# A two-block model on one core: order of two roots, banks of the sums between layers, weight loads three ahead, smaller pieces in the mixing stages, and reordered growth

## The chip, the cores and the metric

The kernel runs on one core of a Trainium2 chip. The metric is the device time of one execution in microseconds (us), lower is better. The comparison is between the median of several executions of the kernel before and of the kernel with the change.

## The reference, cut to what matters

The input is a sequence of 1024 tokens with 1024 channels in f32. The first block computes three branches from one normed input (a WKV7 recurrence, a gated convolution of width 31, an attention to 256 memory rows), merges them with three gates, projects, adds the input and norms with `g_final`. The second block has two layers, and the change lies in it and in what joins it to the first:

```
for layer in range(2):
    h = rms_norm_2(x, norm_pre[layer])
    proj = h @ w_in[layer]                       # 32 tiles of 128 columns and one of 32
    y_a = gla_branch(...)                        # 4 heads, gated scan in both directions
    y_b = diff_branch(...)                       # 4 heads: (softmax(q1 k1) - lam softmax(q2 k2)) v, then norm and gate
    y_c = hgrn_branch(...)                       # 4 heads of 64, gated scan in both directions
    y = concatenate([y_a, y_b, y_c]) @ w_out[layer]
    x = x + rms_norm_2(y, norm_post[layer])
```

## The kernel before, in words

**Engines and the plan.** One Python list, `plan`, is written out by generators, and each engine (TensorE, ScalarE, VectorE, GpSimd, and SyncE, which issues most DMAs) walks through that list and issues its own part of every step. So the order of the plan is the order on every engine, and an engine that waits in one step holds up all its later steps. The profile calls the engines PE (with PEld for its weight loads), ACT, DVE, POOL and SP. A `Filler` (L139) wraps a generator and advances it by fractions of a step; `weave` (L160) advances fillers beside a main generator.

**Projections.** `P` (L331) multiplies the normed input, kept as a rounded f32 part `hh` and a bf16 rest `hl`, by one weight tile: 48 matmuls of 128x512, three products (hh by wh, hh by wl, hl by wh). `deep=4` puts 12 matmuls into one step of the plan. Each projection holds a pair of PSUM banks until a later step copies it out. Banks 0 to 3 are `LOWER` (two pairs), 4 to 7 are `UPPER`. A weight tile comes by DMA into one of two staging slots (SP), ACT copies it into one of three split slots (`wh`), and POOL writes the rest (`wl`). `fill` (L909) decides where in the plan a `load` stands: as early as a split slot is free, but for at most two projections beyond the one that has begun (L921, L934). A slot is free from the step with the last matmuls of its projection; the copy on ACT waits for those.

**End of the first block.** `closing` (L660) runs the last eight projections, squares each result on ACT (`stat_sq`) and adds the squares on DVE. Matmuls with a matrix of ones (`stat_most`, `stat_sum`) add over the channels. For the tag `fin` there are two sums: `fin`, whose root belongs to the first block's norm, and `pre0`, whose root serves the second block's first norm. `stat_end` (L1562) takes Ln and Exp of one sum on ACT. Before the change `pre0` is summed and rooted first. Then `norm_pre` (DVE, L2041) and `split` (ACT, then POOL or DVE) make the input `p0`, and the projections begin. `norm_fin` (DVE) writes the first block's result and SP stores it, for use at the end of layer 0.

**Between the layers.** After the closing projections of layer 0, `resid` adds the layer's result to the input, and `stat("pre1", S)` squares and sums it in a pair of `LOWER` banks; that pair is free after the last `norm_pre` of layer 1.

**The mixing stage** (`mix`, L853), once per layer. Two chains run woven into each other, and a third kind of work fills in:
- `attend` (L816) goes through 4 heads x 8 blocks of 128 queries. Per block: `qk` (PE, 4 matmuls of 128x512 f32), two `dmax` (DVE), two `dexp` (ACT, exponentials with sums), `dw` (DVE: reciprocal, a small product, a scaling of 128x1024 by a column, and one fused multiply-add), then for this block one round later `dt` (PE, 8 transposes), `WT` (ACT, two copies), `dv` (PE) and `do` (ACT).
- `scan` (L681) does the gated scans for t = 0 (gla, 4 heads of 32) and t = 1, 2 (hgrn, 2 heads of 64 each). For each t there are seven levels. A level is: `xk` (ACT, two copies of 128x512), `lev` (PE, 4 parts for t = 0, else 2, each of 8 matmul pairs, in a pair of `LOWER` banks), `leve` (DVE, a predicated copy per part) and `grow` (DVE, six products: for each direction the keys, the queries, and the tree of gates). `xk` and `lev` of the next level wait for all six.
- `beside` (L807) makes values, queries and keys of the next head (`dv_ready`, `qk_ready`) and finishes earlier heads (`head_out`), by projections with `deep=4`. How fast it and `scan` advance beside the blocks is set by hand in `PACE` and `BESIDE` (L844, L845).

Of the kernel before, what the change touches and what calls it, by code (L numbers as in the profile page):

```python
# [135 lines left out]
class Filler:  # L136
# [5 lines left out]
    def step(self, n=1.0):  # L142
        self.owed += n
        while self.owed >= 1 and self.live:
            self.owed -= 1
            try:
                next(self.g)
            except StopIteration:
                self.live = False
# [11 lines left out]
def weave(main, *fillers):  # L161
    for stage in main:
        for f, *n in fillers:
            f.step(n[min(stage or 0, len(n) - 1)])


def build(nc, ctx, A, out):
# [163 lines left out]
    def P(key, src, h, n=S, m=128, back=False, among=LOWER, deep=2):  # L331
# [5 lines left out]
        for part in range(steps // deep):  # L337
            yield
# [317 lines left out]
    def closing(tag, w, h):  # L656
# [16 lines left out]
        for t in tags[::-1]:  # L673
# [100 lines left out]
    def dv_ready(L, h):  # L774

        yield from P(("dvp", L, h), A["w_in_2"][L][14 + h], f"p{L}", deep=4)
        do("dv_copy", L, h)
        yield
        two(("dv_turn", L, h), ("dv_turn", L, h))

    def qk_ready(L, h):

        for i in range(2):
            yield from P(("dqk", L, h, i), A["w_in_2"][L][6 + 4 * i + h], f"p{L}", deep=4)
            do("dq_copy", L, h, i)
            yield
            held(("rope", L, h, i), ("rope", L, h, i))
            yield
# [3 lines left out]
    def head_out(L, h):  # L792
# [6 lines left out]
        yield from between(P(("dg", L, h), A["w_in_2"][L][18 + h], f"p{L}", deep=4), None, ("do_norm", L, h))  # L799
# [14 lines left out]
    def attend(L, n):  # L814
# [15 lines left out]
        if n < 32:  # L830
            do("dw", L, h, q)
        yield
        if n:
            for g in range(2):
                do("WT", L, *last, g)
        yield
        if n:
# [7 lines left out]
    BESIDE = ((1, 2, 3, 2, 3, 3, 3, 2), (5, 6, 4, 3, 0, 0, 1, 6), (3, 4, 3, 4, 3, 1, 0, 0), (0, 2, 3, 3, 3, 2, 2, 0))  # L845
# [7 lines left out]
    def mix(L):  # L853
        ahead, pace = Filler(scan(L)), PACE
        first = Filler(norms_fin() if L == 0 else iter(()))
        for g in (dv_ready(L, 0), qk_ready(L, 0)):
            weave(g, (ahead, 1.2), (first, 2.0))
        for n in range(33):
# [3 lines left out]
            for _ in attend(L, n):  # L862
                ahead.step(pace[h])
                other.step(BESIDE[h][q] / 6)
                ahead.step(pace[h])
            if q == 7:
# [5 lines left out]
    for L in range(2):  # L872
        do("small_load", L)
        if L:
            run(stat("pre1", S))
# [13 lines left out]
    for stage, names in (  # L889
# [8 lines left out]
            ("diff", "dv_copy dv_turn dq_copy rope turned qk dmax dexp dw dt WT dv do do_sq do_sum do_rs do_norm dg_sig dg_out")):  # L898
# [22 lines left out]
    fill(2)  # L921
    for i, s in enumerate(plan):
# [11 lines left out]
        fill(begun + 2)  # L934
# [18 lines left out]
    def tensor_program(pe):  # L953
# [373 lines left out]
        def lev(L, t, lv, g, p):  # L1327
# [3 lines left out]
            if (g, p) == (0, 0):  # L1331
# [4 lines left out]
                else:  # L1336
                    pe.wait_ge(*at("grow", L, t, lv - 1))
# [9 lines left out]
        def kt(L, t, d, g):  # L1347
            use = ("kt", L, t, d, g)
            cleared(use)
            pe.wait_ge(*at("grow", L, t, 6))  # L1350
# [171 lines left out]
    def scalar_program(act):  # L1522
# [375 lines left out]
        def xk(L, t, lv):  # L1898
# [5 lines left out]
            else:  # L1904
                if lv > 1:
                    act.wait_ge(*at("lev", L, t, lv - 2, 1, 1 if t == 0 else 0))
                act.wait_ge(*at("grow", L, t, lv - 1))
# [74 lines left out]

        def WT_(L, h, q, g):
# [28 lines left out]
        def dg_sig(L, h):  # L2012
# [10 lines left out]
                    sg_sig=sg_sig, dv_copy=dv_copy, dv_turn=dv_turn, dq_copy=dq_copy, dexp=dexp, WT=WT_, do=do_, do_sq=do_sq,  # L2023
# [12 lines left out]
    def vector_program(dve):  # L2036
# [396 lines left out]
        def grow(L, t, lv):  # L2433
# [4 lines left out]
            m = 1 << lv  # L2438
            for d in range(2):
# [455 lines left out]
```

## Time and profile before

| | us |
|---|---|
| median of three runs (lowest, highest) | 4501.37 (4494.43, 4509.14) |
| the profiled execution's own time | 4500.21 |
| its span in the trace | 4498.4 |
| mean granted TensorE clock of that execution | 0.931 of full speed |

The profiled execution lies within 1.2 us of the median, and its span leaves 1.8 us around it. In the profile the first block takes until about 2418 us, the mixing stage of layer 0 about 2440 to 3350, that of layer 1 about 3490 to 4450. Times in a timeline are counted from the span's start. In its rows the number behind the start is the length of the merged piece, the brackets give the idle time of that engine before it and what ended it. Matmuls in plain f32 stand as two instructions each.

### The profile page before, as it was taken

The page shows a single profiled execution, that of the slowest core. Times are in us where ns is not written, and L with a number is a line of the kernel's source. Part 1 is how long each engine was busy: PE and PEld are TensorE (multiplying, and loading weights), DVE is VectorE, ACT ScalarE, POOL GpSimd, SP SyncE. Part 2 cuts the span into 40 slices and gives each one's busy share as a digit, 9 for nine tenths or more (in the row PEclk, how much of TensorE's full clock was granted, in tenths as well). Part 3 has the DMA queues.
Part 4 walks back from the last instruction along what each step waited for, and adds up shares of the span by engine and source line. Part 5 has one row for each costly group of instructions (what it writes and reads, how often), then busy time and mean ns, then how long its engine had stood idle before and what let it go on. Part 6 is the DMA issues. An engine that isn't in the chain of part 4 may idle for free.

```text
span 4498.4 us, 66792 instructions
## 1 busy us (share of the span) xinstructions
PE 3923.6 (87%) x29404; PEld 2409.6 (54%) x29404; DVE 1992.3 (44%) x2165; ACT 1439.2 (32%) x1795; POOL 958.7 (21%) x426
## 2 busy tenths in 40 slices
PE   6988899999989999988997978988787978978777
PEld 3555565666656665455444555555444455555444
DVE  2456455555454642432224354263642264264542
ACT  4222323233232322222113323333444232343442
POOL 2313333232333322031132201111002210111002
PEclk8999999999999999999998988989888989989899
DMA  2111111111111112432212000100012100100002
GB/s 92 53 39 39 48 39 53 39 53 45 43 50 42 57 49 84 159 122 103 104 69 86 30 10 19 33 15 24 19 52 76 34 10 10 43 19 20 24 8 101
DMA packets 61585, 226.93 MB, mean 50 GB/s; under 512 B 6832, under 2 KB 8560, under 8 KB 60784
## 3 DMA queue, kind: packets, MB, share of 16 engines
q1 hardware_dynamic: 50064, 181.77, 11.7%
q10 hardware_dynamic: 11232, 40.90, 2.3%
q8 instruction: 231, 3.78, 0.3%
q14 instruction: 58, 0.48, 0.0%
HBM read 174.93 MB, written 47.71 MB: 49 GB/s over the span
## 4 chain that ended last, share of the span: by engine, by line
PE 71%; DVE 16%; ACT 9%; DMA 2%; issue 1%; POOL 1%; ACTq 0%; DVEq 0%; SPq 0%; POOLq 0%
PE psum L955 69%; DVE arena L2038 6%; ACT arena L1524 5%; DVE arena L2041 4%; DVE arena L2493 2%; DVE arena L2430 2%; PE psum L958 2%; ACT L1524 1%; ACT wh L1524 1%; DMA arena<-in_w_proj_conv 1%; DVE arena L2045 1%; ACT arena L1979 1%; DVE hl L2038 0%; ACT hh L1524 0%; POOL wl L2548 0%
## 5 line engine op out<-in xcount | busy, mean ns | idle before, releaser
L955 PE MATMUL psum<-arena 64*64 64x32 f32 (+11 forms) x19116 | 1589.3, 283 | 390.4 <-ACT arena L1524 186.2
L955 PEld LDWEIGHTS psum<-arena 64*64 64x64 f32 (+5 forms) x19116 | 1109.5, 158 | 878.5 <-issue 448.8
L2548 POOL TENSOR_TENSOR wl<-arena,wh 128x1024 bf16<-128x1024 f32 (+1 forms) x195 | 474.7, 2434 | 2405.4 <-ACT wh L1524 2403.6
L955 PE MATMUL psum<-hh,wh 128*128 128x512 f32 x3120 | 891.4, 432 | 98.6 <-ACT arena L1524 24.7
L1524 ACT ACTIVATE arena<-psum 128x512 f32<-128x512 f32 (+4 forms) x660 | 415.8, 630 | 1393.7 <-PE psum L955 1055.3
L955 PE MATMUL psum<-hh,wl 128*128 128x512 bf16 x3120 | 784.0, 394 | 1.2 <-POOL wl L2548 1.2
L955 PEld LDWEIGHTS psum<-hh,wh 128*128 128x128 f32 x3120 | 607.0, 200 | 301.7 <-issue 58.6
L2038 DVE TENSOR_TENSOR arena<-psum,arena 128x512 f32<-128x512 f32 (+3 forms) x488 | 319.3, 654 | 973.7 <-PE psum L955 628.1
L955 PE MATMUL psum<-hl,wh 128*128 128x512 bf16 x3120 | 736.0, 383 | 5.6 <-POOL hl L2548 5.5
L2041 DVE SCALAR_TENSOR_TENSOR arena<-arena 128x1024 f32<-128x1024 f32 x356 | 573.9, 1612 | 83.1 <-ACT arena L1524 69.9
L2548 POOL TENSOR_TENSOR arena<-arena 128x1024 f32<-128x1024 f32 (+4 forms) x142 | 362.6, 2553 | 955.1 <-ACT arena L1524 467.9
L955 PEld LDWEIGHTS psum<-hl,wh 128*128 128x128 bf16 x3120 | 301.7, 99 | 382.2 <-issue 30.2
L955 PEld LDWEIGHTS psum<-hh,wl 128*128 128x128 bf16 x3120 | 277.2, 97 | 414.3 <-issue 98.9
L2038 DVE TENSOR_TENSOR arena<-arena 128x512 f32<-128x512 f32 (+9 forms) x478 | 361.9, 757 | 265.9 <-ACT arena L1524 139.9
L1524 ACT ACTIVATE wh<-arena 128x1024 fp32r<-128x1024 f32 (+1 forms) x195 | 205.1, 1052 | 819.9 <-PE psum L955 538.0
L1524 ACT ACTIVATE arena<-arena 128x1024 f32<-128x1024 f32 (+3 forms) x282 | 253.3, 898 | 389.3 <-DVE arena L2038 217.3
L2493 DVE TENSOR_REDUCE arena<-psum 128x1 f32<-128x1024 f32 x128 | 156.8, 1225 | 318.8 <-PE psum L955 310.8
L2041 DVE SCALAR_TENSOR_TENSOR arena<-psum,arena 128x1024 f32<-128x1024 f32 (+2 forms) x73 | 83.3, 1141 | 412.2 <-ACT arena L1524 251.1
L1524 ACT ACT_TABLE_LOAD x151 | 193.7, 1283 | 57.7 <-PE psum L955 39.2
L1979 ACT ACTIVATE arena<-psum,arena 128x1024 f32<-128x1024 f32 x128 | 142.6, 1114 | 204.3 <-DVE arena L2493 195.9
L958 PE MATMUL psum<-arena 128*128 128x128 f32 x928 | 144.6, 302 | 55.8 <-ACT arena L1524 18.6
L2430 DVE COPY_PREDICATED arena<-arena,psum 128x1024 f32<-128x1024 int32 x112 | 148.7, 1327 | 66.7 <-PE psum L955 60.9
(38 smaller groups left out, 834.1 us busy)
## 6 DMA issues: line engine op xcount, KB each, us to landing
arena<-in_w_in SPq DMA_DIRECT2D x161, 512.0 KB, 3.5
scr_g<-arena ACTq DMA_DIRECT2D x24, 512.0 KB, 2.6
arena<-scr_g SPq DMA_DIRECT2D x24, 512.0 KB, 4.4
arena<-in_w_out SPq DMA_DIRECT2D x24, 512.0 KB, 3.5
arena<-in_w_mem_kv SPq DMA_DIRECT2D x16, 512.0 KB, 3.5
scr_x<-arena SPq DMA_DIRECT2D x16, 512.0 KB, 3.6
arena<-scr_x SPq DMA_DIRECT2D x16, 512.0 KB, 7.4
arena<-in_x SPq DMA_DIRECT2D x8, 512.0 KB, 10.3
```

What stands on the lines that cost most here:

```text
L955: return pe.e.matmul(o, l, r, start=start, stop=stop)
L958: return pe.e.matmul(o, i, ident if idn is None else idn, start=True, stop=True, is_transpose=True)
L1524: return act.seq.activation(o, i, func, bias=bias, scale=scale)
L1979: act.seq.activation(EX[z] if c == 0 else EX[2], pair(use), AF.Exp, bias=s[:, c:c + 1], scale=-1.0, accum_out=s[:, 4 + c:5 + c]).then_inc( ...
L2038: return dve.seq.tensor_tensor(o, a, b, op)
L2041: return dve.seq.scalar_tensor_tensor(o, a, s, b, op0, op1)
L2045: return dve.seq.tensor_scalar(o, a, s1, None, op0)
L2430: dve.seq.copy_predicated(AT8(p, g), mk, cols3(pair(use), 8)).then_inc(*dve.up("ATl", *use))
L2493: dve.seq.tensor_reduce(s[:, c:c + 1], pair(use), AX.X, MIN).then_inc(*dve.up("dmax", L, h, q, c))
L2548: return pool.seq.tensor_tensor(o, a, b, op)
```

## The change

1. In `closing` the sums and roots are made for `fin` first and then for `pre0`. `consts2`, the DMA that overwrites their buffers, now waits for the sum of `pre0`.
2. `stat("pre1")` between the layers takes its pair of banks from `UPPER`.
3. `fill` may place loads for three projections beyond the one begun. The numbers of slots (two staging, three split) stay.
4. In the mixing stages the projections of `beside` use `deep=1`, 3 matmuls per step, each step counted as a quarter; the other steps of `dv_ready` and `qk_ready` that only wait count as a half. `beside` is advanced twice per step of `attend`, by half each time, and `BESIDE` has new numbers. `first` (the first block's `norm_fin`) begins two steps earlier.
5. `dw` is split: `dr` (DVE, the reciprocal and the small product), `e1` (ACT, the scaling of 128x1024, which was on DVE) and `dw` (DVE, the fused multiply-add). They stand in three successive steps of `attend`; `e1` stands behind `WT` of the block before.
6. In `grow` the six products go keys, keys, queries, queries, tree, tree. `xk` waits for the second, `lev` for the fourth; the transposes `kt` wait for the second.

```diff
     def step(self, n=1.0):
         self.owed += n
         while self.owed >= 1 and self.live:
-            self.owed -= 1
             try:
-                next(self.g)
+                self.owed -= next(self.g) or 1
 ...
 def weave(main, *fillers):
-    for stage in main:
-        for f, *n in fillers:
-            f.step(n[min(stage or 0, len(n) - 1)])
+    for share in main:
+        for f, n in fillers:
+            f.step(n * (share or 1))
 ...
-        for t in tags[::-1]:
+        for t in tags:
             do("stat_sum", t)
             do("stat_end", t)
 ...
     def dv_ready(L, h):
-        yield from P(("dvp", L, h), A["w_in_2"][L][14 + h], f"p{L}", deep=4)
+        yield from P(("dvp", L, h), A["w_in_2"][L][14 + h], f"p{L}", deep=1, share=0.25)
         do("dv_copy", L, h)
-        yield
+        yield 0.5
         two(("dv_turn", L, h), ("dv_turn", L, h))
 ...
-            yield from P(("dqk", L, h, i), A["w_in_2"][L][6 + 4 * i + h], f"p{L}", deep=4)
+            yield from P(("dqk", L, h, i), A["w_in_2"][L][6 + 4 * i + h], f"p{L}", deep=1, share=0.25)
             do("dq_copy", L, h, i)
-            yield
+            yield 0.5
             held(("rope", L, h, i), ("rope", L, h, i))
-            yield
+            yield 0.5
 ...
-        yield from between(P(("dg", L, h), A["w_in_2"][L][18 + h], f"p{L}", deep=4), None, ("do_norm", L, h))
+        yield from between(P(("dg", L, h), A["w_in_2"][L][18 + h], f"p{L}", deep=1, share=0.25), None, None, None, ("do_norm", L, h))
 ...
         if n < 32:
-            do("dw", L, h, q)
+            do("dr", L, h, q)
         yield
         if n:
             for g in range(2):
                 do("WT", L, *last, g)
+        if n < 32:
+            do("e1", L, h, q)
         yield
+        if n < 32:
+            do("dw", L, h, q)
 ...
-    BESIDE = ((1, 2, 3, 2, 3, 3, 3, 2), (5, 6, 4, 3, 0, 0, 1, 6), (3, 4, 3, 4, 3, 1, 0, 0), (0, 2, 3, 3, 3, 2, 2, 0))
+    BESIDE = ((1, 1.9, 2.1, 2.1, 2.1, 2.2, 2.4, 2.6), (5, 5, 4, 3, 0, 0, 4, 4), (3, 3, 3, 3, 2, 1, 1, 1.4), (1, 2, 3, 3, 3, 2, 2, 0))
 ...
         first = Filler(norms_fin() if L == 0 else iter(()))
+        first.step(2)
 ...
                 ahead.step(pace[h])
-                other.step(BESIDE[h][q] / 6)
+                other.step(BESIDE[h][q] / 12)
                 ahead.step(pace[h])
+                other.step(BESIDE[h][q] / 12)
 ...
         if L:
-            run(stat("pre1", S))
+            run(stat("pre1", S, UPPER))
 ...
-    fill(2)
+    fill(3)
 ...
-        fill(begun + 2)
+        fill(begun + 3)
 ...
-                    pe.wait_ge(*at("grow", L, t, lv - 1))
+                    pe.wait_ge(*at("grow_q", L, t, lv - 1, 1))
 ...
-            pe.wait_ge(*at("grow", L, t, 6))
+            pe.wait_ge(*at("grow_k", L, t, 6, 1))
 ...
-                act.wait_ge(*at("grow", L, t, lv - 1))
+                act.wait_ge(*at("grow_k", L, t, lv - 1, 1))
 ...
+        def e1(L, h, q):
+            z = q % 2
+            act.wait_ge(*at("dr", L, h, q))
+            f(EX[z], EX[z], AF.Copy, scale=DST[:, 16 * z + 6:16 * z + 7]).then_inc(*act.up("e1", L, h, q))
 ...
+            T, n = [tree(d, lv) for d in range(2)], 512 >> lv
             for d in range(2):
-                T = tree(d, lv)
-                tt(half(KG[d], d, m), half(KG[d], d, m), T[:, :, 1 - d:2 - d].to_broadcast([128, 512 >> lv, m]), MUL).then_inc(*dve.up("grow_k", L, t, lv, d))
-                tt(half(QF[d], 1 - d, m), half(QF[d], 1 - d, m), T[:, :, d:d + 1].to_broadcast([128, 512 >> lv, m]), MUL).then_inc(*dve.up("grow_q", L, t, lv, d))
-                x = tt(tree(d, lv + 1, True).unsqueeze(2), T[:, :, 0:1], T[:, :, 1:2], MUL)
-                x.then_inc(*dve.up(*(("grow", L, t, lv) if d else ("grow_0", L, t, lv))))
+                k = half(KG[d], d, m)
+                tt(k, k, T[d][:, :, 1 - d:2 - d].to_broadcast([128, n, m]), MUL).then_inc(*dve.up("grow_k", L, t, lv, d))
+            for d in range(2):
+                q = half(QF[d], 1 - d, m)
+                tt(q, q, T[d][:, :, d:d + 1].to_broadcast([128, n, m]), MUL).then_inc(*dve.up("grow_q", L, t, lv, d))
+            for d in range(2):
+                tt(tree(d, lv + 1, True).unsqueeze(2), T[d][:, :, 0:1], T[d][:, :, 1:2], MUL).then_inc(*dve.up("grow_t", L, t, lv, d))
 ...
-        def dw(L, h, q):
+        def dr(L, h, q):
             z = q % 2
             s = DST[:, 16 * z:16 * z + 16]
             dve.wait_ge(*at("dexp", L, h, q, 1))
             dve.seq.reciprocal(s[:, 6:8], s[:, 4:6]).then_inc(*dve.up("dw_rec", L, h, q))
-            tt(s[:, 8:9], s[:, 7:8], sc[:, 4:5], MUL).then_inc(*dve.up("dw_lam", L, h, q))
-            ts(EX[z], EX[z], s[:, 6:7], None, MUL).then_inc(*dve.up("dw0", L, h, q))
+            tt(s[:, 8:9], s[:, 7:8], sc[:, 4:5], MUL).then_inc(*dve.up("dr", L, h, q))
+
+        def dw(L, h, q):
+            z = q % 2
+            s = DST[:, 16 * z:16 * z + 16]
+            dve.wait_ge(*at("e1", L, h, q))
             stt(EX[z], EX[2], s[:, 8:9], EX[z], MUL, ADD).then_inc(*dve.up("dw", L, h, q))
 ...
         def consts2():
-            sp.wait_ge(*at("stat_sum", "fin"))
+            sp.wait_ge(*at("stat_sum", "pre0"))
```

## Rows read from the trace of the kernel before

**Rows 1.** The page: busy time, share of the span and instructions of each engine.
```profile
PE 3923.6 (87%) x29404; PEld 2409.6 (54%) x29404; DVE 1992.3 (44%) x2165; ACT 1439.2 (32%) x1795; POOL 958.7 (21%) x426
```
**Rows 2.** Busy time by stretch: first block, mixing stage of layer 0, of layer 1.
```profile
core 0: us, PE busy (x) PEld busy (x) DVE busy (x) ACT busy (x) POOL busy (x), PEclk, DMA share, GB/s
0.00:2400.00 2400.00, 2208.18 (x19607) 1360.06 (x19608) 1074.22 (x1067) 662.18 (x816) 674.51 (x307) 0.97 0.19 66
2540.00:3340.00 800.00, 650.56 (x4013) 415.75 (x4012) 389.19 (x484) 301.26 (x406) 80.01 (x33) 0.87 0.06 18
3540.00:4440.00 900.00, 746.51 (x4487) 466.38 (x4486) 415.59 (x504) 340.56 (x444) 106.45 (x45) 0.90 0.08 27
```
**Rows 3.** PE's groups by shape, 2540 to 3340: busy, mean | idle before, releasers.
```profile
L955 PE MATMUL psum<-arena 64*128 64x128 f32 x512 | 45.6, 326 | 49.9 <-ACT arena L1524 31.6 <-DVE arena L2430 13.3 <-DVE arena L2041 3.5
L955 PE MATMUL psum<-arena 32*128 32x128 f32 x512 | 43.7, 326 | 33.2 <-ACT arena L1524 16.8 <-DVE arena L2430 13.8 <-DVE arena L2038 2.6
```
**Rows 4.** Timeline of layer 0, t = 0: `lev`, a piece, `dt`, growth, `xk`.
```profile
2691.66 1.16 PE L955 MATMUL psum<-arena 32*128 32x128 f32 x16 [1.25 <-ACT arena L1524]
...
2696.66 2.77 PE L955 MATMUL psum<-hl,wh 128*128 128x512 bf16 x12
...
2706.72 1.10 PE L958 MATMUL psum<-arena 128*128 128x128 f32 x8 [0.63 <-ACT arena L1979]
...
2706.89 3.28 DVE L2038 TENSOR_TENSOR arena<-arena 128x512 f32<-128x512 f32 x6
...
2710.26 1.29 ACT L1524 ACTIVATE arena<-arena 128x512 f32<-128x512 f32 x2 [2.26 <-DVE arena L2038]
...
2711.69 1.57 PE L955 MATMUL psum<-arena 32*128 32x128 f32 x16 [3.88 <-ACT arena L1524]
...
2715.55 2.08 PE L955 MATMUL psum<-arena 32*128 32x128 f32 x16 [2.29 <-DVE arena L2430]
```
**Rows 5.** DVE's and ACT's groups by shape, 2540 to 3340.
```profile
L2430 DVE COPY_PREDICATED arena<-arena,psum 128x1024 f32<-128x1024 int32 x56 | 74.3, 1327 | 35.0 <-PE psum L955 32.1
L2038 DVE TENSOR_TENSOR arena<-arena 128x512 f32<-128x512 f32 x90 | 62.3, 692 | 43.1 <-PE psum L955 39.5 <-DVE arena L2493 0.5
...
L2045 DVE TENSOR_SCALAR arena<-arena 128x1024 f32<-128x1024 f32 x40 | 29.9, 747 | 45.2 <-ACT arena L1524 43.9
...
L1524 ACT ACTIVATE wh<-arena 128x1024 fp32r<-128x1024 f32 x24 | 25.4, 1059 | 17.0 <-PE psum L955 8.6 <-DMA arena<-in_w_in 6.5
L1524 ACT ACTIVATE arena<-arena 128x1024 f32<-128x1024 f32 x23 | 24.3, 1058 | 8.8 <-DVE arena L2038 5.9 <-DVE arena L2041 2.3
```
**Rows 6.** Timeline between the layers.
```profile
3475.77 1.06 ACT L1524 ACTIVATE hh<-arena 128x1024 fp32r<-128x1024 f32 x1 [1.35 <-DVE arena L2041]
...
3489.14 1.02 ACT L1524 ACTIVATE hh<-psum 128x1024 fp32r<-128x1024 f32 x1 [1.60 <-DVE psum L2041]
...
3489.17 1.22 PE L955 MATMUL psum<-hh,wh 128*128 128x512 f32 x2 [18.19 <-DVE psum L2041]
```
**Rows 7.** Timeline between the blocks, from the two squares to the first projections.
```profile
2416.64 2.24 ACT L1524 ACTIVATE arena<-arena 128x1024 f32<-128x1024 f32 x2 [12.45 <-DVE arena L2038]
...
2423.19 1.09 ACT L1524 ACTIVATE psum<-psum,arena 128x1024 f32<-128x1024 f32 x1 [2.95 <-PE psum L955]
...
2426.67 1.28 ACT L1524 ACT_TABLE_LOAD   x1
...
2430.39 1.06 ACT L1524 ACTIVATE arena<-arena 128x1024 f32<-128x1024 f32 x1
...
2432.76 1.19 PE L955 MATMUL psum<-hh,wh 128*128 128x512 f32 x2 [7.90 <-ACT hh L1524]
```
**Rows 8.** Timeline, start of the mixing stage of layer 0.
```profile
2467.64 1.06 ACT L1524 ACTIVATE wh<-arena 128x1024 fp32r<-128x1024 f32 x1 [8.64 <-DMA arena<-in_w_in]
...
2469.86 3.65 PE L958 MATMUL psum<-arena 128*128 128x128 f32 x16 [13.68 <-ACT arena L1524]
```
**Rows 9.** PE's groups of the first block, 0 to 2400: hh by wh.
```profile
L955 PE MATMUL psum<-hh,wh 128*128 128x512 f32 x1795 | 503.7, 427 | 47.5 <-ACT wh L1524 12.8 <-ACT hh L1524 9.6 <-DVE arena L2038 9.3
```

More of the change, by code:

```diff
@@ L329, in do, with P @@
         plan.append(step)
-    def P(key, src, h, n=S, m=128, back=False, among=LOWER, deep=2):
+    def P(key, src, h, n=S, m=128, back=False, among=LOWER, deep=2, share=None):
         PROJ[key] = (src, h, n, m, back)
@@ L337, in P @@
         for part in range(steps // deep):
-            yield
+            yield share
             if part == 0:
@@ L783, in qk_ready @@
         for i in range(2):
-            yield from P(("dqk", L, h, i), A["w_in_2"][L][6 + 4 * i + h], f"p{L}", deep=4)
+            yield from P(("dqk", L, h, i), A["w_in_2"][L][6 + 4 * i + h], f"p{L}", deep=1, share=0.25)
             do("dq_copy", L, h, i)
-            yield
+            yield 0.5
             held(("rope", L, h, i), ("rope", L, h, i))
-            yield
+            yield 0.5
             do("turned", L, h, i)
@@ L897, in build @@
                      " so_copy so_sum so_rs so_norm sg_sig sg_out"),
-            ("diff", "dv_copy dv_turn dq_copy rope turned qk dmax dexp dw dt WT dv do do_sq do_sum do_rs do_norm dg_sig dg_out")):
+            ("diff", "dv_copy dv_turn dq_copy rope turned qk dmax dexp dr e1 dw dt WT dv do do_sq do_sum do_rs do_norm dg_sig dg_out")):
         for name in names.split():
@@ L2022, in scalar_program @@
                     ga_copy=ga_copy, ga_abs=ga_abs, ga_ln=ga_ln, ga_exp=ga_exp, hz_gate=hz_gate, xk=xk, kt=kt, so_copy=so_copy, so_rs=so_rs,
-                    sg_sig=sg_sig, dv_copy=dv_copy, dv_turn=dv_turn, dq_copy=dq_copy, dexp=dexp, WT=WT_, do=do_, do_sq=do_sq,
+                    sg_sig=sg_sig, dv_copy=dv_copy, dv_turn=dv_turn, dq_copy=dq_copy, dexp=dexp, e1=e1, WT=WT_, do=do_, do_sq=do_sq,
                     do_rs=do_rs, dg_sig=dg_sig)
@@ L2536, in vector_program @@
                     norm_pre=norm_pre, small=small, ga_z=ga_z, ga_min=ga_min, hz_gate=hz_gate, hz_f=hz_f, ks=ks_, diage=diage, qf=qf, leve=leve,
-                    grow=grow, st=st, so_norm=so_norm, sg_out=sg_out, turned=turned, dmax=dmax, dw=dw, do_norm=do_norm,
+                    grow=grow, st=st, so_norm=so_norm, sg_out=sg_out, turned=turned, dmax=dmax, dr=dr, dw=dw, do_norm=do_norm,
                     dg_out=dg_out, resid=resid)
```

## The prediction

> **What bounds the kernel now.** I read the page first: PE is busy for 87% of the span, DVE for 44%, ACT for 32%, POOL for 21% [rows 1]. So the time is PE's work plus what PE waits for, and a busy microsecond on another engine counts only where PE waits for it. The view of busy time by stretch says where PE waits. In the first block it is busy for 2208 of 2400 us, at a granted clock of 0.97. In the mixing stage of layer 0 it is busy for 650.6 of 800 us, in that of layer 1 for 746.5 of 900, at 0.87 and 0.90 [rows 2]. So each mixing stage loses about 150 us to waiting, 303 us together, and something more to the lower clock. DVE is busy there for 49% and ACT for 38%, so neither is the bound: PE stands because of the order of dependent steps, not because an engine is full. The groups by shape then say which steps: the two shapes of `lev` and `diag` carry 49.9 + 33.2 = 83 of the 149 us of idle time in layer 0 [rows 3]. Most of that (31.6 + 16.8 = 48.4 us) is ended by ACT, which is `xk`, 2.6 by growth on DVE, and 27.1 by the predicated copies that give a pair of banks back.
>
> **The change part by part.** The sum is made against the profiled execution, 4500.2 us, 1.2 us below the median.
>
> *Growth.* In the timeline of one level growth takes 3.28 us for six products, `xk` starts 0.09 us behind it and takes 1.29, and `lev` starts at 2711.69, after 3.88 us of idle PE: 4.80 us from the start of growth [rows 4]. The four wide products take 0.69 us by their group's mean [rows 5]; in this level they must take about 0.72, since two narrow ones are in the 3.28. With the new order `xk` starts after two products (1.5 us) and ends at about 2.9, the fourth product ends at 2.9, and `lev` can start at about 3.05. That is 1.75 us less per level. I followed `lev`'s waits in the timeline of layer 0: 16 of its 21 levels begin with a wait of PE for `xk`, so up to 16 x 1.75 = 28 us; some are shorter than 1.75, as the 1.25 us before 2691.66 [rows 4], and lose only themselves. I take 24 us a layer, **48 us** for both. Bounds: 0, if PE only reaches the next wait, the predicated copy of the same pair of banks, sooner; 2 x 51 = 102 us, if every wait for ACT and growth in those groups went.
>
> *Sums between the layers in upper banks.* PE waits 18.19 us until 3489.17, and what ends it is the last `norm_pre`, because the first projection needs the very pair of banks that holds the sum [rows 6]. The first input tile is ready at 3475.77 + 1.06 = 3476.83. With the sum elsewhere PE can start there, 12.3 us earlier. From then to 3490.16 one tile comes every 2 us or so, and the two first projections take them in turn, 8 matmuls per tile, so PE has enough to do: **-12.3 us**. Bounds: -12.3 and -8, if PE waits between tiles.
>
> *Order of the roots.* Now: squares until 2418.88, the sum of `pre0` until the Ln at 2423.19, Exp, a table load at 2426.67, the root of `fin` until 2431.45, and only then ACT's first split and PE at 2432.76 [rows 7]. Afterwards: the sum of `fin` is ready at about 2419.5, while the second square still runs; its root (two table loads of 1.28, 1.09 and 1.06) takes ACT from 2418.95 to 2423.7, beside PE's sum for `pre0`; the root of `pre0` takes the same 4.7 us, to 2428.4; one `norm_pre` (1.29) and one split later PE starts at about 2430.9. **-1.5 us**, between -3 and +3.
>
> *Loads three ahead.* There are still three split slots. With one projection under way and two loaded they are full, so the third load can't stand three projections ahead; it moves only from the begin of the next projection to the end of the last one, in front of the step that copies that projection out. I counted this in the plan before: 58 loads in the branches of the first block and 28 in each mixing stage move so. ACT's copy takes 1.06 us [rows 5], and the copy-out, which frees the banks, comes so much later: 61 us in the first block and 59 us in the mixing stages, if PE always waited for it. In the first block PE waits at the start of hh by wh for only 47.5 us in all, of which 12.8 are for a `wh` that came late [rows 9]; the rest of its time covers the copy. I take **+5 us** for the whole, between -13 and +60. At the end of layer 0's closing the same copy stands before the last square, which PE's sum waits for: **+1.1 us**. DMAs: SP issues the same transfers, for the moved ones earlier; the staging slots still hold them back to two. The wait of 13.68 us at the start of the mixing stage of layer 0 stays: eight `norm_fin`, each with its store on SP, stand in SP's queue before the load whose copy (8.64 us of waiting) stands on ACT before the copy-out that PE needs [rows 8], and the new plan leaves all of these in that order. If it went: -13.
>
> *Smaller pieces.* A piece of 12 matmuls of the projections keeps PE for 2.77 us [rows 4], one of 3 for a quarter, 0.7 us; the same work is spread over four times as many places between steps that wait. Without the level waits (51 us) 98 us of idle time in layer 0 are left, 27.1 of them for a predicated copy [rows 3]. The mean wait of PE is about 2 us, as the 2.29 before 2715.55 [rows 4], and a piece of 0.7 in front of it takes that much off it. A wait that now follows a large piece loses its cover, though: a predicated copy takes 1.33 us [rows 5] and more than one small piece is needed to hide it. I take 15 us a layer, **-30 us**. Bounds: -100 (half of the 98 us a layer), and +30 (the 27.1 us doubled in one layer's worth).
>
> *The scaling on ACT.* It leaves DVE (0.747 us, 32 per layer) and costs ACT as a copy of 128x1024 1.058 us [rows 5]: DVE gets 24 us a layer back, ACT gets 34 more. What hides it: the block is needed by `dt` only three steps of `attend` later. Without that cover it costs 64 x 1.06 = 68 us. Queued behind `e1` on ACT are `do`, `xk` and the loads; DVE's `dw` waits for it, and behind `dw` stand growth and the predicated copies. I take **0**, between -20 and +68.
> The Trainium skill, Perfetto Trace Analysis, Optimizing Scalar/DVE Operations, speaks against this part: an operation with a fast DVE mode should go to ScalarE only where DVE is saturated. The rows agree on the first half (0.747 against 1.058) and DVE is at 49%; by that rule the move is a loss of 0.31 us for 64 blocks, 20 us, and the sum would be 20 higher.
>
> *Clock.* In a `lev` after a wait of 2.29 us 16 matmuls take 2.08 us, in another 1.16 [rows 4]: the lower of the two levels, 1.2 against 2.4 GHz. A mean of 0.87 and 0.90 means 26% and 20% of the time at the lower level, 208 + 180 us. Idle time falls by a quarter (39 of 150 a layer); if the lower level falls alike, some 95 us change level, PE is busy for 0.82 of them and saves up to half, 39 us. Not every instruction scales, and the other engines' chains don't: I take **-16 us**, between 0 and -39.
>
> Sum: -48 -12.3 -1.5 +5 +1.1 -30 +0 -16 = -101.7, and 4500.2 - 101.7 = 4398.5; by the median **4400 us**, 2.3% faster.
>
> **The rivals.** (A) *The order only moves the waits.* PE reaches the predicated copies and the attention's own waits sooner, and small pieces give nothing: half of growth (-24), the two seams (-12.7), the loads +5, clock -5: 4501 - 37 = 4464. For it: 27.1 us a layer already wait for the copies. Against it: DVE and ACT idle for half of the time, so the chain isn't tight everywhere. (B) *DVE and ACT hold each other, and it gets slower.* DVE's `dw` now waits for `e1`, `e1` stands behind `WT`, and `WT` waits for PE's transposes. From `dt` (1.10 us) over `WT`, two copies of the size of `xk`'s, 1.29 [rows 4], to the end of `e1`, 1.06, it is 3.5 us; DVE stands for it, and the `lev` whose pair DVE should free stands too. If that hits 40 of the 64 blocks it costs 140 us, and -102 becomes +38: 4540. It decides from 102 / 3.5 = 29 blocks on. Against it: one step of the woven chains lies between each two of the three, and PE's step is usually through by then. (C) *The change hardly does what it says*: with three split slots the loads come no earlier, the pieces' places are taken by other steps, and only the two seams remain: 4488, which is 0.3% below and at the edge of what can be told apart. (D) *The page's rule*: the scaling is a plain loss of 20 us, everything else as forecast: 4420.
>
> **How the numbers follow.** Forecast 0.47, A 0.24, B 0.07, C 0.09, D 0.13. The range reaches from 4335 (pieces and clock near their good ends) to 4475 (beyond A); B and C lie outside, and a few more in a hundred below. A measurement of this kernel can tell about 0.3% (13.5 us) from no change. Faster by more than that: forecast, A and D, and a third of C, with something for A's worse half: 0.87. Within: 0.07. Slower: 0.06.
>
> **What would show each step.** Right: between the layers PE starts right behind the first split, some 12 us earlier; in a level `xk` starts after two products; idle time of the two `lev` shapes falls from 83 us a layer to about 55; total idle in a mixing stage from 150 to about 110, and PEclk rises to 0.90 or more; the first block stays within 5 us; the wait of 13.7 us stays. Wrong: DVE idle before `dw`, ended by ACT, of more than 30 us a layer (B); more idle time ended by the predicated copy, where growth's went away (A); a first block longer by more than 15 us (loads).

## The result, and the profile after

The kernel before takes 4497.90 us (median of 4 runs), the changed one **4580.65 us** (4576.02 to 4585.66, 4 runs): ratio 1.018, interval [1.0157, 1.0203], 83 us slower. I had given 4400 (4335 to 4475) and a chance of 0.06 to slower. The profiled execution of the changed kernel took 4582.56 us, span 4580.8.

The page's busy line of the changed kernel, which answers to [rows 1]:
```profile
PE 3958.8 (86%) x29404; PEld 2415.2 (53%) x29404; DVE 1934.1 (42%) x2101; ACT 1500.2 (33%) x1849; POOL 948.2 (21%) x426
```
The same 29404 matmuls take 35 us more of PE, and PE stands still for 622 us instead of 575. ACT has 61 us more and DVE 58 less. Most of that is the scaling, moved as planned: DVE's operations of its kind (TENSOR_SCALAR) take 46 us less, and ACT has 64 copies of 1.06 us more and 10 table loads of 1.28 us less.

Busy time by stretch of the changed kernel, the stretches moved to where its stages now lie [rows 2]:
```profile
core 0: us, PE busy (x) PEld busy (x) DVE busy (x) ACT busy (x) POOL busy (x), PEclk, DMA share, GB/s
0.00:2445.00 2445.00, 2224.42 (x19599) 1372.45 (x19600) 1037.98 (x1066) 662.13 (x816) 669.37 (x307) 0.95 0.18 65
2585.00:3395.00 810.00, 653.53 (x4058) 407.56 (x4055) 375.78 (x453) 336.80 (x438) 82.95 (x35) 0.90 0.06 20
3600.00:4525.00 925.00, 759.40 (x4497) 467.07 (x4498) 402.99 (x472) 372.31 (x472) 102.77 (x44) 0.90 0.07 26
```
The first block, which was to stay within 5 us, takes 45 us more for the same work, and its clock has gone from 0.97 to 0.95. The two stretches of the mixing stages hold 45 and 10 more matmuls than those of [rows 2]; measured from a layer's first `dmax` to its last `do` the stages take 806.7 and 808.1 us, before 799.1 and 786.5. They are 8 and 22 us longer where some 47 each were to go (24 for growth, 15 for the pieces, 8 for the clock).

PE's two `lev` shapes in layer 0, busy, mean | idle before, releasers [rows 3]:
```profile
L960 PE MATMUL psum<-arena 32*128 32x128 f32 x512 | 45.6, 328 | 36.7 <-DVE arena L2440 27.6 <-DVE arena L2048 6.0 <-ACT arena L1529 2.9
L960 PE MATMUL psum<-arena 64*128 64x128 f32 x512 | 45.1, 328 | 36.9 <-DVE arena L2440 18.0 <-ACT arena L1529 13.9 <-DVE arena L2048 4.8
```
Idle time ended by ACT fell from 48.4 to 16.8 us, as growth was to bring, but that ended by the predicated copy (L2440, before L2430) rose from 27.1 to 45.6. In all the two shapes went from 83.1 to 73.6.

The timeline between the layers, at PE's first projection [rows 6], and between the blocks, from the squares to PE [rows 7]:
```profile
3538.22 1.19 PE L960 MATMUL psum<-hh,wh 128*128 128x512 f32 x2 [6.00 <-ACT hh L1529]
```
```profile
2463.55 2.24 ACT L1529 ACTIVATE arena<-arena 128x1024 f32<-128x1024 f32 x2 [0.15 <-DVE arena L2048]
...
2470.19 1.06 ACT L1529 ACTIVATE arena<-arena 128x1024 f32<-128x1024 f32 x1
...
2472.61 1.09 ACT L1529 ACTIVATE psum<-psum,arena 128x1024 f32<-128x1024 f32 x1
...
2478.57 1.19 PE L960 MATMUL psum<-hh,wh 128*128 128x512 f32 x2 [6.80 <-ACT hh L1529]
```
Between the layers PE waits 6.00 us instead of 18.19, the forecast 12. Between the blocks it is 15.0 us from the squares to PE, before 16.1. The two seams did what was said. At the start of the mixing stage PE still waits, 9.61 us, behind a `wh` that waits 16.74 us for its transfer [rows 8].

So the loss isn't where I looked. I matched the same steps of the program in both traces; how much later a step starts in the second is called its delay below. At the last step of the first block's recurrence, 1769 us before, the changed kernel is 49 us late; 6 us of that come in the first 30 us, the rest in small jumps. The view of ACT's waits shows what has changed in kind: `wh` copies that wait for PE, in the mixing stage of layer 0 one with 8.6 us before, and now (2590 to 3390) 26 with 173.1 us:
```profile
ACT wh L1529 <- PE psum L960: 173.1, 26, 18.0
...
ACT arena L1529 <- PE psum L960: 72.0, 18, 7.6
```

### The profile page after: what moved, and what is told of

It is laid out like the page before. It is cut to its first block, busy times and chain, and to the rows that moved or that the text cites. A ratio compares the mean times of both kernels' runs of the same rounds, so it can differ in the third digit from the quotient of the medians.

```text
span 4580.8 us, 66844 instructions
## 1 busy us (share of the span) xinstructions
PE 3958.8 (86%) x29404; PEld 2415.2 (53%) x29404; DVE 1934.1 (42%) x2101; ACT 1500.2 (33%) x1849; POOL 948.2 (21%) x426
## 4 chain that ended last, share of the span: by engine, by line
PE 70%; DVE 15%; ACT 11%; issue 1%; POOL 1%; DMA 1%; ACTq 0%; DVEq 0%; SPq 0%; POOLq 0%
PE psum L960 68%; DVE arena L2048 5%; ACT arena L1529 5%; DVE arena L2051 4%; ACT wh L1529 3%; DVE arena L2506 2%; PE psum L963 2%; DVE arena L2440 2%; ACT L1529 1%; POOL wl L2565 1%; ACT arena L1984 1%; DMA arena<-in_w_proj_conv 0%; DVE hl L2048 0%; POOL arena L2565 0%; DVE psum L2051 0%
## 5 line engine op out<-in xcount | busy, mean ns | idle before, releaser
L960 PEld LDWEIGHTS psum<-arena 64*64 64x64 f32 (+6 forms) x19116 | 1103.4, 158 | 905.4 <-issue 439.2
L2565 POOL TENSOR_TENSOR wl<-arena,wh 128x1024 bf16<-128x1024 f32 (+1 forms) x195 | 465.4, 2387 | 2738.7 <-ACT wh L1529 2737.0
L960 PE MATMUL psum<-hh,wh 128*128 128x512 f32 x3120 | 914.4, 438 | 126.9 <-ACT hh L1529 39.7
L960 PE MATMUL psum<-hh,wl 128*128 128x512 bf16 x3120 | 800.7, 398 | 1.1 <-POOL wl L2565 1.1
L960 PE MATMUL psum<-hl,wh 128*128 128x512 bf16 x3120 | 746.4, 385 | 3.7 <-POOL hl L2565 3.7
L2051 DVE SCALAR_TENSOR_TENSOR arena<-arena 128x1024 f32<-128x1024 f32 x356 | 547.7, 1539 | 198.3 <-ACT arena L1529 184.3
L2048 DVE TENSOR_TENSOR arena<-arena 128x512 f32<-128x512 f32 (+9 forms) x478 | 382.1, 799 | 219.7 <-ACT arena L1529 134.2
L1529 ACT ACTIVATE arena<-arena 128x1024 f32<-128x1024 f32 (+3 forms) x346 | 327.2, 946 | 316.0 <-DVE arena L2048 130.9
L963 PE MATMUL psum<-arena 128*128 128x128 f32 x928 | 154.9, 317 | 65.4 <-ACT arena L1984 43.3
L1529 ACT ACT_TABLE_LOAD x143 | 183.5, 1283 | 23.2 <-DVE arena L2051 9.3
L963 PEld LDWEIGHTS psum<-arena 128*128 128x128 f32 x928 | 131.2, 166 | 107.4 <-ACT arena L1984 52.9
```

Of the source, the lines that this page charges most:

```text
L960: return pe.e.matmul(o, l, r, start=start, stop=stop)
L963: return pe.e.matmul(o, i, ident if idn is None else idn, start=True, stop=True, is_transpose=True)
L1529: return act.seq.activation(o, i, func, bias=bias, scale=scale)
L2048: return dve.seq.tensor_tensor(o, a, b, op)
L2051: return dve.seq.scalar_tensor_tensor(o, a, s, b, op0, op1)
L2565: return pool.seq.tensor_tensor(o, a, b, op)
```

## The experiments

All were timed beside the kernel before on their own chip; each ratio is against that kernel. "Before + x" is the kernel before with part x of the diff alone. The parts are called load, growth, pieces (with their shares, paces and the first steps of the filler), split (the scaling on ACT, and `dr`, `e1` and `dw` as three steps), upper banks, roots. I began with the load, because it had the jumps in the first block.

**The changed kernel with loads two ahead.**
```
-    fill(3)
+    fill(2)
...
-        fill(begun + 3)
+        fill(begun + 2)
```


> The kernel after, with loads two ahead again. Theory L (loads): placing each load in front of the copy-out step costs time on ACT and POOL in the first block, so the 49 us by which the traces differ at the first block's end come back and some of the mixing stages' too: about 4505 to 4530. Theory M (mixing stages): the pieces and the split of the softmax weights make the mixing stages slower by themselves: only the first block's part comes back, and the mixing stages keep their 32 us: about 4530 or more.

Measured: 4481.01 us, ratio 0.9961 [0.9944, 0.9978]. The load takes about 100 us in the changed kernel; without it the change is a small gain.

**Before + load.** The two lines above the other way round.

> The kernel before, with loads three ahead alone. Theory L: 4497 + 49 for the first block + 6 for each closing + something for the mixing stages: 4555 to 4590, the first block longer by 45 to 50. Theory M: 4545 to 4550, no loss in the mixing stages.

Measured: 4692.26 us, 1.044 [1.0412, 1.0468]: +194 us, 49 up to the end of the first block's recurrence, the rest in and around the mixing stages. My term for it was +5, with an upper bound of +60.

**Before + growth.**

> The kernel before, with the reordered growth alone. By the prediction's step 48 us faster, 4450 (4440 to 4475), idle time of lev's first parts down from 44 us a layer to 20. Rival: PE only reaches the next wait sooner: 4485 to 4497.

Measured: 4497.85 us, 0.9994 [0.9979, 1.0009]. No gain, although `xk` starts early. One level in its timeline (the fifth of t = 0; [rows 4] shows the growth of the sixth):
```profile
2690.00 3.32 DVE L2038 TENSOR_TENSOR arena<-arena 128x512 f32<-128x512 f32 x6 [1.32 <-PE psum L955]
2691.50 1.29 ACT L1524 ACTIVATE arena<-arena 128x512 f32<-128x512 f32 x2 [3.00 <-DVE arena L2038]
2693.35 1.32 DVE L2430 COPY_PREDICATED arena<-arena,psum 128x1024 f32<-128x1024 int32 x1
2694.72 3.14 PE L955 MATMUL psum<-arena 32*128 32x128 f32 x32 [1.13 <-DVE arena L2430]
```
`xk` starts 1.50 us after growth and ends at 2.79, as worked out. But the predicated copy that gives `lev` its banks stands on DVE behind all six products, and it ends at 4.67. `lev` starts 4.72 us after growth; before it was 4.84 in this level, and in the level of [rows 4] it is 4.69 here and was 4.80. Not every level is like that: by the matched steps 6 of the 36 levels that follow a growth come 1.7 to 2.8 us nearer to it, and all 36 together 19 us. The kernel keeps none of it: in the profiled executions the stage of layer 0 is 6.3 us shorter and that of layer 1 7.1 us longer. The two gates trade places in PE's waits of layer 0's mixing stage, 2540 to 3340 (us, times, longest), first the kernel before, then this one:
```profile
PE psum L955 <- ACT arena L1524: 75.8, 38, 7.0
PE psum L955 <- DVE arena L2430: 33.3, 19, 3.3
```
```profile
PE psum L955 <- DVE arena L2430: 50.2, 28, 4.0
PE psum L955 <- ACT arena L1524: 48.8, 28, 7.0
```

**Before + pieces.**

> The kernel before, with the small pieces, their shares and the new rates alone. By the prediction's step 30 us faster, 4468. Theory M: slower by 15 to 40 us, with more idle time before dt, rope and the first matmuls of projections.

Measured: 4557.39 us, 1.0134 [1.0104, 1.0165]: +59 us by the medians and +58 by the spans of the profiled executions, where I had -30 with a bad end of +30.

These don't add up: 59 for the pieces, nothing for growth, and yet 17 us of gain with all but the load. Two questions followed: which part of the load costs, and which part undoes the cost of the pieces.

**The load by engine.** The plan's one step stands in three queues: SP issues the DMA, ACT copies to `wh`, POOL subtracts to `wl`. I gave the engines a second step at the old place:
```
             moved.append(("load", key))
+            early.append(key)
...
+    def rest(n):
+        while len(late) < min(n, len(early)):
+            moved.append(("load_late", early[len(late)]))
+            late.append(0)
...
-    fill(2)
+    fill(3)
+    rest(2)
...
-        fill(begun + 2)
+        fill(begun + 3)
+        rest(begun + 2)
```
In the first of the two kernels ACT and POOL do their part at `load_late`, in the second POOL alone.

> Loads three ahead alone cost 194 us over the kernel before (49 in the first block, 65 and 80 in the mixing stages). Here only SP issues the DMA three ahead; ACT's wh copy and POOL's wl stay at their old places. If it is the copies' places on ACT and POOL that cost, this is the kernel before within 15 us, with 6 of them in the first microseconds, where the third load stands on SP ahead of the x DMAs and waits for the first one's w_lo. If it is SP (the wait for a staging slot, which holds up every later DMA of its queue), this takes most of the 194 us: about 4650.

> As the one before, but ACT's wh copy stands three ahead too, and only POOL's wl keeps its old place. If ACT's copy in front of the copy-out is what costs (PE waited 180 us for wh copies ended by its own bank release in the mixing stage of layer 0, against 9 before), this takes nearly all of the 194 us: 4650 to 4690. If it is POOL's wl (2.4 us, which stands ahead of POOL's own steps and waits for ACT), this stays near SP's alone: 4500 to 4530, and the rest comes with POOL. My guess: ACT, at least 120 us.

Measured: SP alone 4497.72 us, 0.9996 [0.9981, 1.001]; SP and ACT 4669.07 us, 1.0381 [1.0356, 1.0407]. SP's place costs nothing, **ACT's copy costs about 171 us**, POOL's the 23 that are left. Not all of the 171 us is waiting: between the profiled executions of these two kernels, whose traces hold the same 29104 matmul records, the span grows by 177 us, PE's busy time by 72 of them (3884.0 to 3956.1), at a mean granted clock of 0.915 in place of 0.933, and its idle time by 105.

**Load three ahead, but behind the copy-out.** The slot is given free one step later (the lines that gave it free at once go):
```
             moved.append(s)
+            if ended:
+                if PROJ[ended][1] is None:
+                    free_w.append((place_w[ended], ended))
+                else:
+                    free_s.append((place_s[ended], ended))
             key = ("vm", s[1]) if s[0] == "vmp" else s[1] if s[0] == "proj" else None
+            ended = key if key and last_part[key] == i else None
```

> Loads three ahead on all engines, but a slot counts as free only behind the step that copies the projection out, so ACT's wh copy stands behind that copy-out instead of in front of it. Three ahead in front cost 194 us, of which SP's place cost nothing, ACT's 170 and POOL's about 25. If what costs is that the copy stands in front of the copy-out and waits there for the projection's last matmul, this is within 20 us of the kernel before, with the 6 us of the first microseconds among them. If any early copy costs, because ACT stands at it for a projection's end while its other steps are due, most of the 170 stays: 4620 to 4690.

Measured: 4593.85 us, 1.0208 [1.0189, 1.0226]: between the two: 94 us stay, 100 are gone. The edit isn't a pure one: 79 loads, most of which stood in front of a copy-out in the kernel before already, come one step later than there. The timelines of ACT show what is gone. One gate's copy-out (`sg_sig` of the first head, layer 0), first in the kernel before, then with the load three ahead, then with the load behind:
```profile
2788.90 1.28 ACT L1524 ACT_TABLE_LOAD   x1
2798.02 1.02 ACT L1524 ACTIVATE arena<-psum 128x1024 f32<-128x1024 f32 x1 [7.83 <-PE psum L955]
```
```profile
2864.31 1.06 ACT L1524 ACTIVATE wh<-arena 128x1024 fp32r<-128x1024 f32 x1 [9.26 <-PE psum L955]
2865.45 1.28 ACT L1524 ACT_TABLE_LOAD   x1
2866.74 1.02 ACT L1524 ACTIVATE arena<-psum 128x1024 f32<-128x1024 f32 x1
```
```profile
2835.08 1.02 ACT L1525 ACTIVATE arena<-psum 128x1024 f32<-128x1024 f32 x1 [7.82 <-PE psum L956]
2836.20 1.06 ACT L1525 ACTIVATE wh<-arena 128x1024 fp32r<-128x1024 f32 x1
```
Before, ACT loads its table for the gate while it waits for PE, and the gate starts at once. With the load in front, ACT waits at the `wh` copy for the same projection, and copy and table load come behind the wait: the gate starts 2.43 us after PE instead of at once. A step's new delay is its delay less that of ACT's step before it, the loads left out. `sg_sig`, `hz_gate` and `dg_sig` of both layers, 24 in all, take 20.1 + 23.2 + 23.2 = 66.5 us of new delay, the plain copies of the mixing stages 55 us, mostly 1.1 each, the `spill` copies of the first block 34.3 (28 of the 48 have 1.1 us or more) and `dexp`, which is no copy-out, 32.0. With the load behind the copy-out `hz_gate` takes 2.5 us in place of 23.2. What the other 94 us are was not taken apart: by the same matching they lie on other steps of ACT's queue (`do` 36.8, `close` 20.8, `w0` 19.0, `dexp` 16.9, `sv_copy` 15.7 us).

**Before + split, and before + upper banks + roots.**

> The scaling of the attention block on ACT, and the reciprocal, the scaling and the last product as three steps at three places, alone. The kernel with loads two ahead and everything else is 12 us below the kernel before, although its pieces alone cost 57, its growth nothing and its seam gives 10.5 back. If these only add up, the scaling must be worth some -58: 4440. If the pieces' loss comes from the same waits that the split takes away, the split alone gives less: 4460 to 4490. If DVE and ACT hold each other (rival B), it is slower than before: over 4510. The page's rule gives +20: 4518.

> The sums between the layers in upper banks and the order of the roots, alone. By the term of the prediction -12.3 and -1.5: 4484, ratio 0.997, with PE's wait between the layers down from 18.2 to about 6. If PE only waits for later tiles instead, -8 and 0: 4490. If the later stages take it back, 4498.

Measured: the split 4488.74 us, 0.9982 [0.9969, 0.9995], a gain of 8 by the ratio (10.5 by the medians); the seams 4484.09 us, 0.9967 [0.9955, 0.998], a gain of 15. The split moves the scaling to another engine and its parts to other steps at once; which of the two gives the gain was not separated. The gain at the layers' seam is 12.7 us by the matched steps, from `split` of the first tile to the first copy-out.

**Pairs with the pieces, and everything but pieces and load.**

> The split of the attention's scaling (alone: -8 us) together with the small pieces and their shares (alone: +57). If the two work together, that is, if the small pieces with the old shares of time leave PE without work behind DVE's scaling and the split fills that place, this is at or below the kernel before: 4470 to 4500. If they only add up: 4548. Everything but the loads gave -18, which needs -52 from some such pair; this pair or the next.

> The reordered growth (alone: 0) together with the small pieces (alone: +57). If growth is the partner, because PE reaches the level waits sooner with small pieces and growth then shortens them: 4495 to 4510. If the split is the partner, nothing changes against the pieces alone: 4550 to 4560.

> Growth, the split, the upper banks and the roots; old pieces and loads two ahead. By the single effects (0, -8, -15 for the last two together) 4475 to 4477. If growth gets its gain once the split keeps DVE free (the predicated copy no longer stands behind the scaling), 20 to 40 less: 4440 to 4455, and it beats both kernels and the one with everything but the loads (4481).

Measured: split + pieces 4495.61 us, 0.9988 [0.9978, 0.9997]; growth + pieces 4549.29 us, 1.0108 [1.0093, 1.0123]; growth + split + seams 4474.43 us, 0.9942 [0.992, 0.9964]. So the pieces cost 59 alone and 3 to 7 with the split (by the ratios and by the medians). They never gain: with growth, split and seams they cost 7 (4474.43 against 4481.01), with the DMA three ahead as well, below, 12. That growth takes some of the 59 off isn't shown: 8 us between the medians, and the intervals overlap. Without pieces the single effects add up: 0 + 8 + 15 = 23, measured 25.

What the pieces do is seen in stretches that hold the same work, from the first `dmax` of layer 0 to its last `do` (columns as above), first before + pieces, then before + split + pieces:
```profile
2544.90:3364.90 820.00, 664.41 (x4006) 420.47 (x4052) 408.41 (x484) 296.37 (x402) 82.31 (x34) 0.86 0.06 19
```
```profile
2540.80:3326.90 786.10, 639.89 (x4006) 403.55 (x4052) 379.80 (x452) 333.19 (x434) 82.73 (x34) 0.90 0.06 19
```
The same matmuls (4006 records in both) take 24.5 us less of PE with the split, at a granted clock of 0.90 in place of 0.86; PE's idle time falls by 9.4 (155.6 to 146.2). So most of what the split gives back here is busy time at a higher clock, not waiting. It is so over the whole execution too: of the 69.5 us between the two spans, PE's busy time is 51.1 (3932.3 to 3881.2). For comparison, the kernel before has 798.8 us, PE 650.7, clock 0.87 from its first `dmax` to its last `do`, with 37 fewer weight loads (4015 for 4052). Why the granted clock is lower without the split the runs don't show.

**Why the load costs half as much in the changed kernel.**

> Loads three ahead with the split of the attention's scaling. Loads alone cost 194 us, in the changed kernel with all its parts about 100. The first block's 49 have nothing to do with the split and stay. If the split is what halves the rest (it moves a copy of ACT's into the places where the early wh copies make ACT's steps late, and takes DVE off the path): about 4590 to 4610. If the small pieces halve it, since PE then has something to do at each wait: 4499 + 194 - 8 = 4685. If the split's 1.06 us on ACT add to the loads' 1.05 on ACT: over 4700.

Measured: 4668.03 us, 1.0371 [1.0357, 1.0385]. Load on top of the split costs 179 us, nearly as much as alone. My first guess, that the split halves it, is wrong. With the split, growth, pieces and seams the load costs 100, so one of the other three, or several together, bring it down. I take it to be the pieces, but load + pieces was not run, nor load + growth or load + seams.

**Which version is best.**

> The best version so far (growth, split, upper banks, roots: 4474) without the growth. If growth gives nothing with the split either: 4476, within 0.15% of it. If it gets its gain only with the split: 4485 or more.

> The best version so far, with SP alone issuing the weight DMAs three ahead from the second projection on, so that the wait of 6 us in the first microseconds is gone too, and the 13.7 us wait at the start of layer 0's mixing stage stays, since the stores of the normed tiles still stand ahead on SP. If the weights' transfers are late nowhere else, it is the same: 4474. If the 10 to 20 us that the profile of the SP-only kernel showed in the memory attention and layer 0's mixing stage are real: 4455 to 4465.

Measured: without growth 4480.44 us, 0.9951 [0.9937, 0.9965], so growth gives nothing that can be told apart there either. With SP alone three ahead **4448.81 us, 0.9883 [0.987, 0.9897]**: 25.6 us under the version without it and 53 under the kernel before, the fastest of all. Unlike the first kernel with SP alone three ahead, it starts with two loads. Where the gain comes from, 1770 to 2190 us (merge and memory attention), without and with it (columns as above):
```profile
1770.00:2190.00 420.00, 365.25 (x1392) 215.27 (x1406) 139.85 (x213) 107.97 (x183) 75.23 (x30) 0.94 0.32 116
```
```profile
1770.00:2190.00 420.00, 378.86 (x1471) 221.83 (x1470) 141.60 (x214) 107.98 (x183) 76.69 (x31) 0.96 0.36 129
```
In the same 420 us PE does 13.6 us more and the DMAs move 129 GB/s in place of 116; by the matched steps 19 us are won from 1769 us to the end of the memory attention. SP alone on the kernel before lost 6.8 us at the start, won 16 in this stretch and ended 10 ahead in its profiled execution (span 4488.5, one of its faster ones), while its median shows nothing; why that pair doesn't give as much as this one stays open.

**The changed kernel with only the DMA three ahead.**

> The changed kernel with its weight DMAs three ahead as it has them (from the second projection on), but ACT's wh copy and POOL's wl back at their places of two ahead. Against the kernel before, loads two ahead gave 4481; the DMA's early place gave -25 on the version without the small pieces, of which 20 between 1770 and 2190 us, where the transfers are densest. If that gain doesn't depend on the pieces: 4456, about 125 below the changed kernel, and the whole loss of the change is the place of two copies. If the pieces already hide the late transfers: 4475 to 4481.

Measured: 4460.63 us, 0.9912 [0.9899, 0.9926]. Against the changed kernel it differs in the places of ACT's and POOL's copies and in the start with two loads: 120 us.

| kernel | us | ratio |
|---|---|---|
| before + load | 4692.26 | 1.044 |
| before + load on SP and ACT | 4669.07 | 1.0381 |
| before + load + split | 4668.03 | 1.0371 |
| before + load behind the copy-out | 4593.85 | 1.0208 |
| **the change** | 4580.65 | 1.018 |
| before + pieces | 4557.39 | 1.0134 |
| before + growth + pieces | 4549.29 | 1.0108 |
| before + load on SP alone | 4497.72 | 0.9996 |
| before + growth | 4497.85 | 0.9994 |
| before + split + pieces | 4495.61 | 0.9988 |
| before + split | 4488.74 | 0.9982 |
| before + upper banks + roots | 4484.09 | 0.9967 |
| change, loads two ahead | 4481.01 | 0.9961 |
| before + split + upper banks + roots | 4480.44 | 0.9951 |
| the same + growth | 4474.43 | 0.9942 |
| change, only the DMA three ahead | 4460.63 | 0.9912 |
| growth + split + upper banks + roots + DMA three ahead | 4448.81 | 0.9883 |

## Why the prediction was wrong

The measured loss is the load (+100 on top of the rest) less what the rest gives (-17).

- **Loads three ahead, +5 with bounds -13 and +60: this step failed and decided the sign.** The move itself was read right: 58 and 28 loads go in front of the copy-out, and 21 more in the three closings. I priced each at the copy's own 1.06 us and took PE's idle time at the start of the projections [rows 9] as what is exposed. Both halves were wrong. The copy also pushes the table load of the gates behind the wait (2.43 us, not 1.06), the delays of the copy-outs add up along the whole kernel, where I let PE's other work cover most of them, and loads three ahead cost 94 us even with the copy behind the copy-out (the 6 us of the start and POOL's part are in that). Nor had the term any clock in it: of the first block's 45 us more, 16 are PE busy for longer at a lower clock, and of the 177 us of ACT's copy alone 72. The first block longer by more than 15 us was my own sign that this term is wrong. The 6 us at the start I had not seen at all: a third load on SP ahead of the first input tiles. The bound should have been taken from the delay of each thing queued behind on ACT, not from PE's present idle time at one kind of step.
- **Growth, -48 (bounds 0 and -102): measured 0, by rival A's mechanism.** The price per level was right to 0.1 us for `xk`, but `lev` has two gates, and in most levels the second, the predicated copy, was late by the same amount (4.69 us for 4.80 in the level of [rows 4]). Six levels of 36 did gain 1.7 us and more, and PE met that time again at later waits. I named it as the lower bound, "if PE only reaches the next wait, the predicated copy of the same pair of banks, sooner", and took a value in the middle. The row with 2.29 us before a `lev`, ended by that copy [rows 4], had shown it.
- **Pieces, -30 (-100 to +30).** Alone +59, beyond the bad end; with the split +3 to +7. The reason given, that a piece of 0.7 us takes that much off a wait, doesn't hold: in the stretch of layer 0 PE's idle time did not fall but rose from 148.1 to 155.6 us (up to 4.6 of it may be matmul records that are missing), and the waits for predicated copies from 33.3 to 45.2 in the view of PE's waits. PE's busy time rose by 13.7 as well, which says little, since the stretch holds 37 more weight loads. What makes up the 59 us was not taken apart.
- **The split, 0 (-20 to +68): -8 alone.** It costs no time on ACT that shows. DVE does wait for ACT before `dw`, 49.4 us in layer 0 of the changed kernel and 87.4 in the one with the split alone, more than the 30 that I had named as the sign of rival B; yet that kernel is no slower. That sign was chosen badly: idle time of an engine that isn't the bound. The rule that I weighed as rival D (the Trainium skill, Perfetto Trace Analysis, Optimizing Scalar/DVE Operations) would have made it, as I priced it, a loss of 20; with DVE at 49% and ACT at 38% it was a gain of 8 alone, and of 62 on top of the pieces (4557.39 to 4495.61). The measurement decides against it here. That the single operation is slower on ACT the rows do show (1.058 against 0.747); a loss for the kernel did not follow from it.
- **Upper banks, -12.3, and roots, -1.5:** 18.19 to 6.00 and 16.1 to 15.0 us in the trace, 15 us together in the median. Right.
- **Clock, -16:** the mixing stages have the clock that I asked for (0.90 in both) and no gain in time, and the first block lost 0.02.

Of the rivals, A was right on growth, and B, the only slower one, was slower for a reason that did not cost. None of the four had the load as its mechanism.

## What to carry to other kernels

When a step that several engines take part in is moved, price it queue by queue: what stands behind it on each, and what that engine used to do while it waited (here a table load of 1.28 us that was free). Moving only the transfer was worth 20 and 26 us in two versions and nothing in the kernel before; moving the copies with it cost 120 in the changed kernel. And where a step waits for two things, shortening one is worth nothing until the timeline shows how late the other is.

## What the runs showed of the hardware

ACT can perform a table load ahead of an instruction that still waits for its semaphore (2788.90, gate at 2798.02), and there it is free; put another instruction that waits before it, and it is paid in full (2865.45). It isn't always so: in the kernel before all 24 gates have the table load in front of their wait, but 9 `spill` copies have it behind, as at 331.75, after 11.14 us of waiting for PE, with the copy at 333.05. What tells the two cases apart the runs don't show; the timeline has to be read for each. Not expected either: the same matmuls of layer 0's stage took 24.5 us more of PE at a clock of 0.86 than at 0.90, so a change in the order of small steps that takes 9 us off the idle time can be worth another 3% of a stage.
